# Order of the scores on TensorE and of the exponents on ScalarE in the attention stage

## The reference, cut to what matters

```python
for i in range(s // Q_BLOCK):                      # 8 blocks of 128 queries
    end = (i + 1) * Q_BLOCK
    sc = einsum('bhcqd,bhckd->bhcqk', q[..., q0:end, :], k[..., :end, :]) * scale
    prob = softmax(where(causal, sc, neg), axis=-1)
    attn = prob[:, :, 0] - lam * prob[:, :, 1]     # c = 0 and c = 1
    blocks.append(einsum('bhqk,bhkv->bhqv', attn, v[:, :, :end]))
```

## Time and profile before

| | |
|---|---|
| Median of 3 runs | 3435.37 us (3434.65 to 3440.79) |
| The profiled execution | 3437.85 us |
| Its span, first to last instruction | 3436.0 us |
| PE busy in the span | 2939.7 us (86%), 21224 instructions |
| PEld, DVE, ACT, POOL busy | 2516.8, 1899.9, 1274.7, 728.9 us |
| Mean granted clock of TensorE | 0.911 |

### The profile page before, as it was taken

The page is one execution under the profiler, slowest core; times in us unless marked ns, Lnnn a source line. Parts: engine busy times, 40 slices in busy tenths (PEclk is TensorE's granted clock), DMA queues, the critical chain, the costliest instruction groups (busy, mean ns, idle before and its releaser), DMA issues. The chain is left out here.

```text
span 3436.0 us, 53128 instructions
## 1 busy us (share of the span) xinstructions
PE 2939.7 (86%) x21224; PEld 2516.8 (73%) x21224; DVE 1899.9 (55%) x2335; ACT 1274.7 (37%) x1812; POOL 728.9 (21%) x469
## 2 busy tenths in 40 slices
PE   8999978896685895599999959799999895957699
PEld 7999976776353785488878847699999774744487
DVE  3365736774573334488888846410178675665421
ACT  3000005563554222377777734211111265532311
POOL 3222303331360000222222100133233140220000
PEclk9999998997687997799999979899999996888899
DMA  5464331100314533699999953333566713041421
GB/s 185 166 210 174 128 108 43 35 29 29 69 62 166 183 111 130 219 392 399 398 399 399 398 194 115 137 132 121 170 197 214 254 44 143 7 144 33 178 98 49
DMA packets 256460, 572.34 MB, mean 167 GB/s; under 512 B 25904, under 2 KB 99760, under 8 KB 254688
## 3 DMA queue, kind: packets, MB, share of 16 engines
q1 hardware_dynamic: 207744, 456.45, 37.0%
q10 hardware_dynamic: 37936, 74.40, 5.9%
q0 software_dynamic: 10608, 39.13, 3.6%
HBM read 442.28 MB, written 126.45 MB: 166 GB/s over the span
## 5 line engine op out<-in xcount | busy, mean ns | idle before, releaser
L385 PE MATMUL pin_psum<-pin_sb_w,pin_sb_hT 128*128 128x354 f32 (+1 forms) x5376 | 979.4, 344 | 15.6 <-DVE pin_sb_hT L331 5.8
L385 PEld LDWEIGHTS pin_psum<-pin_sb_w,pin_sb_hT 128*128 128x128 f32 x5376 | 940.2, 190 | 52.1 <-DVE pin_sb_hT L331 6.3
L4233 DVE TENSOR_TENSOR moe_sb_wlo<-moe_sb_raw,moe_sb_whi 128x2048 fp32r<-128x2048 f32 x192 | 437.9, 2288 | 94.0 <-ACT moe_sb_whi L4058 93.7
L4058 ACT ACTIVATE moe_sb_whi<-moe_sb_raw 128x2048 fp32r<-128x2048 f32 x192 | 367.4, 1916 | 135.4 <-DMA moe_sb_raw<-in_w_gate 47.4
L308 ACT ACTIVATE pin_sb_xt<-pin_psum,pin_sb_ss 128x353 f32<-128x353 f32 (+1 forms) x112 | 63.7, 589 | 564.1 <-PE pin_psum L385 494.4
L360 DVE TENSOR_SCALAR pin_sb_xt<-pin_psum,pin_sb_ss 128x353 f32<-128x353 f32 (+1 forms) x112 | 69.0, 625 | 331.2 <-PE pin_psum L385 331.0
L4301 PE MATMUL moe_psum<-moe_sb_whi,moe_sb_xhi 128*128 128x512 f32 x512 | 205.0, 400 | 15.7 <-DVE moe_sb_xlo L4237 15.7
L261 POOL CAST pin_sb_w<-pin_sb_raw 128x2832 fp32r<-128x2832 f32 (+1 forms) x26 | 75.2, 2894 | 633.5 <-PE pin_psum L385 588.5
L4301 PE MATMUL moe_psum<-moe_sb_whi,moe_sb_xlo 128*128 128x512 f32 x512 | 201.6, 394 | 0.0
L4301 PE MATMUL moe_psum<-moe_sb_wlo,moe_sb_xhi 128*128 128x512 f32 x512 | 201.5, 394 | 0.0
L263 POOL TENSOR_TENSOR pin_sb_w<-pin_sb_raw,pin_sb_w 128x2832 fp32r<-128x2832 f32 (+1 forms) x26 | 186.9, 7189 | 3.9 <-issue 0.7
(11 more groups left out here) (698 smaller groups left out, 5681.7 us busy)
## 6 DMA issues: line engine op xcount, KB each, us to landing
moe_sb_raw<-in_w_gate SPq DMA_DIRECT2D x64, 1024.0 KB, 12.4
moe_sb_raw<-in_w_up SPq DMA_DIRECT2D x64, 1024.0 KB
moe_sb_raw<-in_w_down SPq DMA_DIRECT2D x64, 1024.0 KB, 12.6
scratch_proj<-pin_sb_xt ACTq DMA_DIRECT2D x16, 1412.0 KB, 6.4
scratch_proj<-pin_sb_xt ACTq DMA_DIRECT2D x12, 1792.0 KB, 6.2
pin_sb_raw<-in_w_in SPq DMA_DIRECT2D x15, 1412.0 KB, 7.2
pin_sb_raw<-in_w_in SPq DMA_DIRECT2D x11, 1792.0 KB, 8.9
scratch_ybuf<-moe_sb_yb ACTq DMA_DIRECT2D x32, 512.0 KB, 6.8
```

The source lines that it names most:

```text
L385: mm = te.matmul(ps[:, t, 0:cols], hT[a_part][:, k, t * P:(t + 1) * P], wt[b][w_part][:, k, :], start=(k == 0 and n == 0), stop=(k == KD - ...
L4058: s.activation(whi[q][:, :, :], raw[q][:, :, :], ACT.Copy).then_inc(hi, 1)
L4233: tt(wlo[q][:, :, :], raw[q][:, :, :], whi[q][:, :, :].bitcast(F32), ALU.subtract).then_inc(lo, 1)
```

## The change

On PE, scores(i+2) are issued ahead of flatten(i, 0) and not behind it. Where step i+2 is narrow that holds for both components; where it is wide, for component 0 alone, and component 1 stays behind flatten(i, 0). On ACT, where step i+1 is narrow, weigh(i+1, 1) goes ahead of flatten(i, 0), right behind weigh(i+1, 0); where it is wide the order stays. The work of DVE, POOL and SP, the buffers and the waits in front of each piece of work are the same.

```diff
--- before.py
+++ after.py
@@ -2220,8 +2220,10 @@
             for i in range(STEPS):
                 if i + 1 < STEPS:
                     weigh(i + 1, 0)
+                if i + 1 < STEPS and narrow(i + 1):
+                    weigh(i + 1, 1)
                 flatten(i, 0)
-                if i + 1 < STEPS:
+                if i + 1 < STEPS and not narrow(i + 1):
                     weigh(i + 1, 1)
                 if rounds(i) > 1:
                     flatten(i, 1)
@@ -2322,14 +2324,14 @@
             mm.then_inc(turned0, 1)
             te.wait_ge(kept, 1)
 
-            def scores(i):
+            def scores(i, parts=pair):
 
                 t, h = i // AH, i % AH
                 if t:
                     te.wait_ge(kept, i - AH + 2)
                 q = lambda c: qkT[64 * c:64 * c + 64, 0, h, t * P:(t + 1) * P]
                 k = lambda c: qkT[64 * c:64 * c + 64, 1, h, 0:width(i)]
-                for c in pair:
+                for c in parts:
                     for j, cc in before(i, c):
                         te.wait_ge(weighed, 2 * j + cc + 1)
                     if narrow(i):
@@ -2369,9 +2371,12 @@
             scores(0)
             scores(1)
             for i in range(STEPS):
+                ahead = i + 2 < STEPS
+                if ahead:
+                    scores(i + 2, pair if narrow(i + 2) else (0,))
                 flatten(i, 0)
-                if i + 2 < STEPS:
-                    scores(i + 2)
+                if ahead and not narrow(i + 2):
+                    scores(i + 2, (1,))
                 if rounds(i) > 1:
                     flatten(i, 1)
                 output(i)
```

## The result

| | before | after |
|---|---|---|
| Median of 6 runs each, same chip | 3437.11 us (3430.52 to 3444.34) | 3457.81 us (3452.03 to 3461.81) |
| Ratio, 95% interval | | 1.0051 (1.0039 to 1.0064) |
| The profiled execution | 3437.85 us | 3452.03 us |
| Attention, PE's first to last instruction in it | 211.5 us (854.4 to 1065.9) | 231.5 us (851.7 to 1083.2) |
| Mean granted clock of the profiled execution | 0.911 | 0.905 |

A forecast was written before the change was run, and what follows sets the result against it. No engine is full in the narrow steps; a loop of turned blocks, scores and DVE's work sets their period. Narrow -3.0 plus wide +1.7 gave -1.3 us, so 3434.1 us from the 3435.37 median; 8 in 10 for 3428.5 to 3441.

The forecast's parts named there:

- Part 1, narrow: Narrow steps, scores of i+2 ahead of the turned blocks: sum -3.0 us, bounds none or at most 15.5 us.
- The ring: ACT's narrow-step loop (keep, exponents, copy, output): 3.94 us against 4.09 at width 256, 3.18 against 3.06 at 128.
- Two signs that I named: Narrow steps: DVE's wait for scores, 26.6 us, falls below 10; ACT's wait for output grows by about one exponent.
- Parts 2 and 3, the passage: Step 13's copy +0.65 us; step 14's turned blocks, copy and output behind the scores' exponent wait, output 4 us later.
- the cover: Step 15: PE waits until 947.08 anyway for DVE's 6.25 us operation, hiding delays and leaving +1.6 us in step 16.
- The three lost pairs: Steps 14, 15 and 16: components no longer side by side at 1.2 GHz, a loss of about 2.1 us each.
- a sign of being wrong that I had named: Step 15: the forecast is wrong if a long DVE operation, 6.25 us before, no longer covers it.
- Part 4, the lost pairs: Wide steps: components no longer side by side, 10.5 us lost but partly covered by waits; wide sum +1.7 us.
- Part 5: Steps 19 to 22 and 27 to 30: PE full or waiting for an unmoved ACT table load, so 0.
- rival A: Clearly faster: PE's waits for `mix` vanish (a third: 3426 us) or some steps reach 2.4 GHz (3425.4 us); chance 0.12.
- the forecast of busy time: Wide steps: PE's busy time up by about 8 us.
- Rival B: Slower: step 15's wait no longer hides the lost pairs, those of 24 and 25 too; +9.2 us, 3444.6 us; chance 0.08.

The follow-up runs named there:

- a7: The change plus four unread matmuls on the array's other half beside component 0 of steps 16 to 25; 3432.14 us, 0.9980 of the kernel before.
- c1: a7 again, unaltered, on a fourth chip; 3438.08 us, 0.9989 of the kernel before.
- a6: The change plus two unread 128 by 128 matmuls in PE's wait before each output of steps 14 to 22; 3435.58 us, 0.9992 of the kernel before.
- c4: a7 with the narrow steps in the old order, ACT taking both exponents first only in step 14; 3445.18 us, 1.0020 of the kernel before.
- a2: The change in the narrow steps alone, wide scores in the old place behind the turned blocks; 3438.05 us, 0.9992 of the kernel before.
- c2: The change a third time, unaltered, on the fourth chip; 3456.67 us, 1.0035 of the kernel before.
- b4: The change once more, not a line altered, in the third series; 3442.65 us, 1.0011 of the kernel before.

## Why the prediction was wrong

*Part 1, narrow: right in time.* The ring gave width 256 a period of 3.94 us; from `keep(4)` to `keep(5)` it is 3.93 (877.84 to 881.77). Step 5's blocks came 0.8 us and step 8's 1.8 us earlier. Width 128 became longer, as forecast: keep to keep 3.18 us (863.99 to 867.17) in the timeline of the kernel after, the sum of the ring to the hundredth:

```profile
863.99 0.37 ACT L2206 ACTIVATE att_sb_o<-att_psum,att_sb_rs 128x128 f32<-128x128 f32 x1 [1.38 <-PE att_psum L2367]
...
865.01 0.35 ACT L2191 ACTIVATE att_sb_e<-att_psum,att_sb_mn 128x128 f32<-128x128 f32 x1
...
865.69 0.27 ACT L2200 ACTIVATE att_sb_aT<-att_psum 128x128 f32<-128x128 f32 x1
...
867.17 0.37 ACT L2206 ACTIVATE att_sb_o<-att_psum,att_sb_rs 128x128 f32<-128x128 f32 x1 [1.21 <-PE att_psum L2367]
```

By step 13 the sum was -3.4 against my -3.0. Two signs that I named were wrong all the same: VectorE's wait for scores fell only from 26.6 to 20.7 us, not below 10, and ScalarE's wait for the output did not grow (22.0 before, 21.5 after). PE's 21.3 us for `mix` did go, to one start-up wait of 5.4, and came back for the most part in the wait for the copy, 15.5 us where it had been 3.0. The ring tells the period, but not which engine shows the slack.

*Parts 2 and 3, the passage: right in time.* I had the turned blocks of step 14 at 932.3 in the old time, 5.7 later than their 926.6; less the 3.0 that I had won before, that is 2.7, and they came 2.5 later. Step 15's were 2.4 later, and step 16's 1.5 earlier, for my 1.6 - 3.0 = -1.4. But the cover was not there as I had drawn it. DVE's one-column operation took 2.49 us at 937.40, not 6.25, and `at` of step 16 was ready at 940.85. PE asked for it only at 942.84, because component by component at 1.2 GHz it worked from 923.97 on without a gap of its own. The three lost pairs had used up the old wait of 6.95 us, as the sum said, and how long DVE's operation takes no longer mattered. So a sign of being wrong that I had named came true and cost nothing.

*Part 4, the lost pairs: right from step 23 on, short at step 18.* No four 512-column instructions run in 1.1 us any more in the wide steps. From step 23 to 26, where I let the pairs of 24 and 25 come out even with the waits, it took 21.2 us against 21.0. PE's wait for `mix` in the wide steps fell from 12.3 to 1.6 us. From step 17 to 18, where my sum had 0.4 us, 3.4 were lost. The wait of 3.15 us for ACT's exponent behind the table loads stands there, of which I had only that the loads swallow 0.3. The filled kernel a7, with the same order and 3.09 us of the same wait, lost 1.0 there (10.2 against 9.2 us), so the rest went with the clock.

*Part 5, "Steps 19 to 22 and 27 to 30 have PE full: 0": this step failed.* I put this term at nothing, and it cost 18.1 us between the blocks of step 18 and those of step 23, at 1.2 GHz in place of 2.4. The same assumption stands in rival A as "the steps from 968 on are at the high level already". I took the clock of each step over from the old trace as if it belonged to the step, and asked only whether the change could raise it in steps 14 to 17. PE full is just where a change of level costs most: nothing covers it, and the instructions take nearly twice as long (four turned blocks 0.66 before, 1.11 after). The sign that would have asked the question was in my own rows: the earlier trace rows has both levels in one stage, and the earlier trace rows show that the change makes two instructions at once into one at a time. In the forecast of busy time it shows as well: I had it up by 8 us, and 45.97 + 109.42 = 155.4 became 46.01 + 137.51 = 183.5. The rest of the sum had the right sign: with the clock back, the stage took 208.9 us in a7 and 208.3 in c1, 2.6 and 3.2 less than before, where I had 1.3 less.

Rival B had the right sign, its 3444.6 us not half of the loss, and another mechanism; no run was a case of it: a7 and c1 lost the same pairs and had a shorter stage than before. Rival A's point about the clock held with the opposite sign.

The Trainium skill, "TensorE: Matmul & The Clock Gate", section "The HAM clock gate", has the clock follow how busy the engine has lately been. Read as busy time in the profile, this case disagrees: PE was busy 15.00 of 15 us and stayed at 1.2 GHz. The same section warns that the events of the gate in a trace can be unreliable, and reports one seen stuck at a quarter of the clock for over 50 us. Here the instructions' own times bear the level out (2.07 us for what took 1.12), it was a half and not a quarter, and it went with the order of work: filler in the same order brought 2.4 GHz back.

**What stays open.** The low level is shown to be the loss, and filler to take it away; what in the split sets it is not shown. Why the change was long in 6 of 6, 5 of 12 and 9 of 12 executions: the chips differed, and so did the moment at which the stage begins, and I have not parted the two. Whether it is the half of the array that decides or the work in it altogether: a7 fills the other half, a6 uses whole matmuls in short waits, and the profiles of both have the high level. Why the same filler won nothing in c4. And the narrow gain: -0.08% in a2, which is no more than can be measured, so its share in a7's 0.2% is not shown.

## What to carry to other kernels

The clock level of a stretch is not a property of the step; it can change with what PE runs there and just before: before costing a reordering at zero in a stretch where PE is full, ask what it would cost at the other level, and give that a chance. Be wary of moving matmuls that use half of the rows apart when they ran side by side; where it has to be done, work on the other half that costs nothing is worth a trial, in several executions and not in one: a7 was 0.2% faster than the kernel before, its repetition c1 0.1% with an interval that takes in 1, and in c4 the filler won nothing. A loss that comes in some executions only is read from the sorted times with their clocks, not from a median of three.

## What the runs showed of the hardware

- PE, busy with no gap or nearly none, stayed at 1.2 GHz: 15.00 of 15 us from 925 to 940, 14.63 of 15 from 970 to 985, both at 0.50, where the kernel before had 13.68 of 15 at 1.00.
- Four instructions of 64 rows by 128 columns on the other half of the rows ran entirely beside one of 512 columns (0.61 beside 0.59 us, a7), and they are all that differs between the kernels c2 and c1, whose profiled executions have 0.54 and 0.87 over the same 75 us.
- A wait of PE of about 3 us, begun at 2.4 GHz, was followed by 1.2 GHz: 3.15 us in the kernel after, 3.09 in a7. With filler the high level was back in about 3 us (2.34 us for the ten instructions at 955.51, 0.66 for four turned blocks at 959.56); without it PE ran from 955 to 994 at the low one.
- One and the same program, on one chip, fell in two groups (b4: seven from 3429 to 3445, five from 3454 to 3461 us, their medians 18.6 us apart). On another chip the same program showed no such gap (c2).
